# Outer norms of the mixing block and the memory attention computed by token halves, with GpSimd adding their residuals and squares

## The reference, cut to what matters

```python
x = x + rmsnorm(y @ w_out[l], g_mix_post[l])      # (1) mix_post
h = rmsnorm(x, g_mem_pre[l])                      # (1) mem_pre
y = memory_cross_attention(h, mem_n, w_mq[l], w_mk[l], w_mv[l], w_mo[l])
x = x + rmsnorm(y, g_mem_post[l])                 # (2) mem_post
h = rmsnorm(x, g_ff_pre[l])                       # (2) ff_pre
y = jnp.square(jax.nn.relu(h @ w_ff1[l])) @ w_ff2[l]
x = x + rmsnorm(y, g_ff_post[l])
```

## Time and profile before

| | us |
|---|---|
| median of 3 runs (2120.17 to 2122.87) | 2120.91 |
| profiled execution: time | 2122.2 |
| profiled execution: span of the core | 2120.4 |
| seam 1, last two blocks of w_out to the closing of mem_pre | 309.67 to 353.66 |
| seam 2, last two blocks of w_mo to the closing of ff_pre | 440.78 to 484.77 |

### The profile page before, as it was taken

How to read it: one execution, slowest core, us unless ns; L and a number is a source line. 1 busy time by engine, 2 the same in 40 slices (tenths; PEclk the granted TensorE clock), 3 DMA queues, 4 the chain that set the end, 5 groups by cost and what they waited for, 6 DMA issues and landing times.

```text
span 2120.4 us, 27323 instructions
## 1 busy us (share of the span) xinstructions
PE 2074.9 (98%) x11100; PEld 1665.4 (79%) x11100; DVE 1243.8 (59%) x1943; ACT 836.3 (39%) x1362; POOL 210.8 (10%) x182
## 2 busy tenths in 40 slices
PE   8999999999999999999999999999999999999998
PEld 7787977678878886666988888887777779888887
DVE  5566746446677777986644344475675756443443
ACT  5345544445323233225523223354464455232232
POOL 1321011011000004552000000100000010000002
PEclk9999999999999999999999999999999999999999
DMA  6313422016677762763232333121121232323331
GB/s 203 116 53 100 150 93 86 20 60 217 219 278 255 260 232 90 181 166 93 97 104 96 100 100 100 54 70 51 60 70 51 70 106 94 104 96 100 100 100 40
DMA packets 219710, 245.56 MB, mean 116 GB/s; under 512 B 9272, under 2 KB 205368, under 8 KB 213440
## 3 DMA queue, kind: packets, MB, share of 16 engines
q1 hardware_dynamic: 209360, 231.20, 33.3%
q10 hardware_dynamic: 10224, 12.61, 2.3%
HBM read 237.75 MB, written 3.78 MB: 114 GB/s over the span
## 4 chain that ended last, share of the span: by engine, by line
PE 88%; DVE 5%; ACT 3%; DMA 2%; issue 1%; ACTq 0%; POOL 0%; DVEq 0%; SPq 0%
PE bank L1420 24%; PE bank L1424 24%; PE bank L1428 24%; PE bank L1446 2%; PE bank L1454 2%; PE bank L1450 2%; PE bank L1556 1%; PE bank L1630 1%; DVE wL L2039 1%; PE bank L1607 1%; PE bank L1514 1%; PE bank L1491 1%; PE bank L1499 1%; ACT wH L1666 1%; PE bank L1620 1%
## 5 line engine op out<-in xcount | busy, mean ns | idle before, releaser
L1420 PE MATMUL bank<-hH,wH 128*128 128x512 f32 (+1 forms) x1768 | 643.7, 385 | 15.8 <-ACT wH L1671 7.9
L1428 PE MATMUL bank<-hL,wH 128*128 128x512 f32 (+1 forms) x1768 | 627.0, 375 | 0.0
L1424 PE MATMUL bank<-hH,wL 128*128 128x512 f32 (+1 forms) x1768 | 626.5, 375 | 0.0
L1666 ACT ACTIVATE wH<-raw 128x1024 fp32r<-128x1024 f32 (+1 forms) x376 | 333.8, 937 | 365.3 <-PE bank L1428 293.1
L2039 DVE TENSOR_TENSOR wL<-raw,wH 128x1024 fp32r<-128x1024 f32 (+1 forms) x340 | 378.8, 1151 | 136.3 <-ACT wH L1666 136.2
L1420 PEld LDWEIGHTS bank<-hH,wH 128*128 128x128 f32 x1768 | 326.6, 189 | 101.7 <-issue 28.0
L1428 PEld LDWEIGHTS bank<-hL,wH 128*128 128x128 f32 x1768 | 327.1, 189 | 60.7
L1424 PEld LDWEIGHTS bank<-hH,wL 128*128 128x128 f32 x1768 | 326.9, 189 | 60.0 <-issue 3.1
L1420 PE MATMUL bank<-hidH,wH 128*128 128x512 f32 (+1 forms) x800 | 305.1, 381 | 1.9 <-ACT hidH L1830 1.9
L1428 PE MATMUL bank<-hidL,wH 128*128 128x512 f32 (+1 forms) x800 | 304.6, 381 | 0.0
L1424 PE MATMUL bank<-hidH,wL 128*128 128x512 f32 (+1 forms) x800 | 304.4, 381 | 0.0
(11 more groups left out here) (220 smaller groups left out, 2037.1 us busy)
## 6 DMA issues: line engine op xcount, KB each, us to landing
raw<-in_mlp SPq DMA_DIRECT2D x64, 1024.0 KB, 5.3
araw<-in_ada_w SPq DMA_DIRECT2D x48, 1024.0 KB, 5.1
raw<-in_w_ff SPq DMA_DIRECT2D x32, 1024.0 KB, 7.3
raw<-in_hgrn_in SPq DMA_DIRECT2D x32, 512.0 KB, 3.7
raw<-in_w_in SPq DMA_DIRECT2D x11, 1024.0 KB, 5.2
raw<-in_conv_in SPq DMA_DIRECT2D x16, 512.0 KB, 3.9
u<-conv_u ACTq DMA_DIRECT2D x24, 270.0 KB, 5.1
raw<-in_w_mv SPq DMA_DIRECT2D x4, 1024.0 KB, 5.0
```

What stands on the lines that cost most here:

```text
L1420: mm(out, wH[:, s, m:m + 128], xh[:, k, c], start=k == 0, stop=False)
L1424: mm(out, wL[:, s, m:m + 128], xh[:, k, c], start=False, stop=False)
L1428: i = mm(out, wH[:, s, m:m + 128], xl[:, k, c], start=False, stop=k == KB - 1)
L1666: do(wH[:, s, c], raw[:, r, c], ACT.Copy).then_inc(*s_whi.up(n, x))
```

## The change

Both seams get the halved form; `post_norm` replaces the second branch of `post_pre`. All eight `post_x` of both halves go to POOL. All eight squares of the next norm are put off until the second half has been scaled, and all seven additions go to POOL. The three useless matmuls go from these two closings. `beside` is called after `between` and the next weight's high part. Half keys are renamed from 0 to "a", which changes no instruction. Left out below are the same half slices in `ev_block`, `pre_hi`, `pre_lo` and `post`.

```diff
@@ linear @@
-            if self.beside is not None:
-                self.beside()
-                self.beside = None
...
                     if k == 1:
                         between()
                         self.highs(ns[0] + NSPLIT)
+                        if self.beside is not None:
+                            self.beside()
+                            self.beside = None
@@ post_pre, post_norm @@
-            self.close(tag, 1024, busy=BUSY)
-            add = {}
-            for j in range(KB):
-                self.do("post", tag=tag, src=src, j=j, rb=None, z=None)
-                if j:
-                    self.do("pre_lo", tag=tag, nxt=nxt, j=j - 1)
-                self.do("post_x", tag=tag, src=src, j=j, pool=False, z=None)
-                self.do("pre_hi", tag=tag, nxt=nxt, j=j)
-                if j < 4:
-                    self.to_add = None
-                    self.square(nxt, j, ("xT", j), (self.x_event(tag, j),), by="dve")
-                    add[j + 2], self.to_add = self.to_add, None
-                if add.get(j) is not None:
-                    self.do("add_square", **add[j])
-            self.do("pre_lo", tag=tag, nxt=nxt, j=KB - 1)
-
-            def rest():
-                for j in range(4, KB):
-                    self.square(nxt, j, ("xT", j), (self.x_event(tag, j),))
-            self.beside = rest
+    def post_norm(self, tag, nxt):
+
+        def scale(half):
+            for j in range(KB):
+                self.do("post", tag=tag, src="ymix", j=j, rb=None, z=None, half=half)
+                if j:
+                    self.do("pre_lo", tag=tag, nxt=nxt, j=j - 1, half=half)
+                self.do("post_x", tag=tag, src="ymix", j=j, pool=True, z=None, half=half)
+                self.do("pre_hi", tag=tag, nxt=nxt, j=j, half=half)
+                yield
+            self.do("pre_lo", tag=tag, nxt=nxt, j=KB - 1, half=half)
+
+        def squares():
+            for j in range(KB):
+                self.square(nxt, j, ("xT", j), (self.x_event(tag, j),))
+
+        def second():
+            self.close_half(tag, 1024, 1)
+            run(scale(1))
+            self.rstd_free = (("dve", "post", tag, KB - 1),)
+            self.beside = squares
+
+        return dict(close=lambda half: self.close_half(tag, 1024, half), scale=scale, second=second)
@@ build @@
-        run(self.linear("w_out", "w_out", 0, 0, 1024, ("h", "y"), to_block("mix_post"), fresh=2))
-        self.post_pre("mix_post", "mem_pre", "ymix")
+        mem_pre, ff_pre = self.post_norm("mix_post", "mem_pre"), self.post_norm("mem_post", "ff_pre")
+        run(self.linear("w_out", "w_out", 0, 0, 768, ("h", "y"), to_block("mix_post"), fresh=2))
+        run(self.seam("w_out", "w_out", 0, 0, ("h", "y"), to_block("mix_post"), mem_pre))
...
         run(self.linear("mq", "w_mq", 0, 0, 1024, ("h", "mem_pre"), to_mq,
-                        before=lambda: self.close("mem_pre", 1024), fresh=4, hold=5))
+                        before=lambda: self.close("mem_pre", 1024), fresh=4, hold=5, between=mem_pre["second"]))
...
-        run(self.linear("w_mo", "w_mo", 0, 0, 1024, ("h", "mo"), to_block("mem_post"), fresh=2))
-        self.post_pre("mem_post", "ff_pre", "ymix")
+        run(self.linear("w_mo", "w_mo", 0, 0, 768, ("h", "mo"), to_block("mem_post"), fresh=2))
+        run(self.seam("w_mo", "w_mo", 0, 0, ("h", "mo"), to_block("mem_post"), ff_pre))
...
-        run(weave(self.ffn("ff_pre", "w_ff1", 0, "w_ff2", 0, ("h", "ff_pre"), True, to_y), ada(), RM, start=-12.0))
-        self.post_pre("ff_post", None, "yff")
+        run(weave(self.ffn("ff_pre", "w_ff1", 0, "w_ff2", 0, ("h", "ff_pre"), True, to_y, between=ff_pre["second"]), ada(), RM,
+                  start=-12.0))
+        self.post_pre("ff_post", "yff")
@@ pool_program, post_x @@
-                    e.tensor_tensor(xT[:, j, :], xT[:, j, :], y, ADD).then_inc(*s_pool.up("x", tag, j))
+                    e.tensor_tensor(xT[:, j, c], xT[:, j, c], block(it["src"], j)[:, c], ADD).then_inc(
+                        *s_pool.up("x", tag, j, *end))
```

More of the change, by code:

```diff
@@ L176, in cols @@
         return slice(0, T), ()
-    return (slice(0, T // 2), (0,)) if half == 0 else (slice(T // 2, T), ())
+    return (slice(0, T // 2), ("a",)) if half == 0 else (slice(T // 2, T), ())
 class Schedule:
@@ L401, in close_half @@
                 rstd_free=() if half else self.rstd_free, out=out, half=half)
[L402 removed]
+        self.lin.put(b, ("act", "ln", tag, *cols(half)[1]))
         if half:
@@ new lines, in second, with post_pre @@
+        def second():
[4 more added lines that the diff above has]
+        return dict(close=lambda half: self.close_half(tag, 1024, half), scale=scale, second=second)
+    def post_pre(self, tag, src):
+        rb, free = self.lin.get()
+        self.close(tag, 1024, busy=BUSY, out=(rb, free))
+        for j in range(KB):
+            pool = j in BY_POOL
+            z, free = (None, ()) if pool else self.lin.get()
+            self.do("post", tag=tag, src=src, j=j, rb=rb, z=z, after=free, half=None)
+            self.do("post_x", tag=tag, src=src, j=j, pool=pool, z=z, half=None)
+            if not pool:
+                self.lin.put(z, ("dve", "x", tag, j))
+        for j in range(KB):
+            self.square_mm(tag, j)
+        self.lin.put(rb, ("dve", "post", tag, KB - 1))
@@ L562, in scale @@
     def scale(self, tag, before, half):
-        end = (0,) if half == 0 else ()
+        end = cols(half)[1]
         held = None
@@ L1435, in tensor_program @@
                     wl = wL[:, n % NSPLIT, :].rearrange("p (b n) -> p b n", b=KB)
-                    ready = (0,) if it.get("half") == 0 else ()
+                    ready = cols(it.get("half"))[1]
                     for k in it["ks"]:
@@ L2163, in vector_program @@
                     tag, j = it["tag"], it["j"]
[L2164 to L2166 removed]
+                    c, end = cols(it["half"])
+                    y = block(it["src"], j)[:, c]
+                    dve.wait_ge(*s_act.at("rstd", tag, *end))
+                    dve.wait_ge(*(s_dve.at("y", 3, j) if tag == "ff_post" else s_act.at("y", tag, j, *(end if j >= KB - 2 else ()))))
                     for ev in it.get("after", ()):
                         dve.wait_ge(*event(ev))
[L2169 to L2171 removed]
+                    e.scalar_tensor_tensor(out=y if it["z"] is None else banks[it["z"]][:, c], in0=y, scalar=vc(GAIN[tag], j),
+                                           in1=rstd[:, c] if it["rb"] is None else banks[it["rb"]][:, c], op0=MUL,
+                                           op1=MUL).then_inc(*s_dve.up("post", tag, j, *end))
                 elif kind == "post_x" and not it["pool"]:
@@ L2174, in vector_program @@
                     dve.wait_ge(*s_dve.at("post", tag, j))
[L2175 to L2178, removed]
+                    dve.wait_ge(*event(plan.x_event("mem_post", j)))
                     z = block(it["src"], j) if it["z"] is None else banks[it["z"]][:]
                     e.tensor_tensor(xT[:, j, :], xT[:, j, :], z, ADD).then_inc(*s_dve.up("x", tag, j))
[L2181 to L2185, removed]
                 elif kind == "pre_lo":
                     j = it["j"]
[L2188 to L2191, removed]
+                    c, end = cols(it["half"])
+                    dve.wait_ge(*s_hi.at(it["nxt"], j, *end))
+                    dve.wait_ge(*event((*plan.x_event(it["tag"], j), *end)))
+                    e.scalar_tensor_tensor(out=hL[:, j, c], in0=xT[:, j, c], scalar=vc(GAIN[it["nxt"]], j),
+                                           in1=hH[:, j, c].bitcast(F), op0=MUL, op1=SUB).then_inc(
+                        *s_lo.up(it["nxt"], j, *end))
                 elif kind == "ev_mq":
@@ L2480, in pool_program @@
                     tag, j = it["tag"], it["j"]
-                    y = block(it["src"], j)
-                    pool.wait_ge(*s_dve.at("post", tag, j))
+                    c, end = cols(it["half"])
+                    pool.wait_ge(*s_dve.at("post", tag, j, *end))
                     if tag == "mix_post":
```

38 lines of the change are left out of this document (13 added, 25 removed).

## The result

The changed kernel takes 2136.93 us (median of 5 runs, 2134.21 to 2137.81), the kernel before 2120.91 us (median of 5, 2120.17 to 2122.87). The ratio is 1.0068, with a 95% interval of 1.0057 to 1.0079: the change makes the kernel slower by 12 to 17 us. The prediction said 2133.5 us in a range of 2121.5 to 2138, with 80% for slower. The profiled execution has a span of 2132.3 us.

A forecast was written before the change was run, and what follows sets the result against it. PE, busy 98% of the span, was taken as the bound. Per seam +5.7 us (late closing) and +0.6 (clock) gave +6.3, for both +12.6 on the median 2120.91: 2133.5 us, range 2121.5 to 2138.

The forecast's parts named there:

- What bounds: At two seams: PE is busy 98% of the span, so its idle time and number of matmuls decide the change's worth.
- PE alone: Per seam, without waits: mem_pre's closing sum at t = 41.4 from block 5's end instead of 43.99, a gain of 2.6 us.
- The first half's chain: In each seam: DVE, POOL and ACT need 1.42 us a block against PE's 1.44; PE waits 0.8 us at second closing.
- The start of the additions: Late in each seam, after the squares begin: POOL starts the first of seven additions at t = 37.2; last ends at 49.6.
- The closing: Next norm's closing sum: PE, there at t = 42.2, waits for POOL until 49.7, 5.7 us later than 43.99.
- The clock: After PE's wait at each seam's closing: a fall of the granted clock costs 0.6 us, bounds 0 and 1.4.
- The sum: Both seams: +5.7 and +0.6 make +6.3 us a seam, +12.6 in all, giving 2133.5 us.
- PE alone decides: Rival, 7%: POOL is ready for both closings and PE runs through; -2.6 us a seam, 2115.8 us.
- The turns at the end: From the fourth addition, POOL additions and DVE low parts alternate, 2.25 us a pair; rival lacking turns or hold-up: 12%, 2127.2.
- the hold-up within the chains: In halved chains, a DVE operation behind a POOL one loses 0.5 us; rival lacking this or the turns: 12%, 2127.2.

The follow-up runs named there:

- the repeat: The changed kernel measured once more, unaltered, beside the kernel before: 2138.51 us against 2123.77, ratio 1.0069.
- the filled one: The changed kernel plus seven useless matmuls ahead of the closing sums of mem_pre and ff_pre, in PE's wait: 2135.22 us, ratio 1.0055; again 2134.01, ratio 1.0052.

## Why the prediction was right

- **What bounds**: right. PE's idle time at two places decided it; with the additions off GpSimd the rest of the change gains, and with the additions alone the kernel loses.
- **PE alone**: predicted t = 41.4 for a closing without waits, measured 41.96. The narrow matmuls cost what the earlier trace rows gave (7.20 us to the first sum, to the digit). Of the 0.56 us missing, 0.2 lie in the second halved sum, 0.90 us instead of 0.68, and the rest in small steps before and behind it.
- **The first half's chain**: of the 0.8 us of wait at the second closing only those 0.2 came. The square of block 7 started at 323.79, t = 15.4, where I had 15.9: the first `post` started at t = 9.2 instead of 9.4, and ACT, POOL and DVE each handed on a little sooner than I had written out. The block's distance was 1.42 us in the sum and 1.39 in the trace. The hold-up of DVE came out at 0.47 to 0.48 us, as in the earlier trace rows (`post` of 0.95 and 0.96 us beside an addition), and not at POOL's whole 0.73. The Trainium skill says that the two engines exclude each other, and for the whole instruction (SBUF — State Buffer, "Who interferes with whom"), and the trace agrees: each `post` that is held up ends 0.28 to 0.29 us behind POOL's addition, as here at 325.37 and 325.08. What DVE loses is what is left of the addition when DVE gets to its own instruction. The prediction had read the rule as a loss of the whole 0.73 us, 1.53 a block; that doesn't follow from it.

```profile
324.18 0.90 POOL L2488 TENSOR_TENSOR xT<-xT,vt 128x256 f32<-128x256 f32 x1 [0.84 <-DVE vt L2176]
324.42 0.95 DVE L2176 SCALAR_TENSOR_TENSOR vt<-vt,vec,rstd 128x256 f32<-128x256 f32 x1
```

- **The start of the additions**: t = 37.2 predicted, 36.1 measured (344.46), the same small steps added up (Ln of the second half at t = 21.0 instead of 21.6, its first `post` at 21.9 instead of 22.7). Their length: 12.4 us predicted, 12.50 measured, with the turns. The last one ended 1.0 us sooner than I had it, and that is the error of this term.
- **The closing**: +5.7 us a seam predicted, +4.7 measured.
- **The clock**: the term that was mis-sized. I put 0.6 us a seam, between bounds of 0 and 1.4 from the earlier trace rows. It cost 3.8 and 2.4 us in one execution, 2.4 twice in the other. I had reasoned that part of a short low phase would lie within the wait. But the phases were 13.7 and 10.2 us long, where the one of the earlier trace rows lasts 3.4, and 9 and 6 us of them lay behind the wait:

```profile
352.53:366.19 13.66, 8.25 (x17) 5.37 (x18) 8.59 (x8) 1.32 (x2) 4.14 (x3) 0.50 0.46 154
492.48:502.70 10.22, 5.04 (x9) 2.91 (x10) 6.77 (x6) 2.80 (x5) 4.06 (x2) 0.50 0.62 205
```

- **The sum**: 12.6 us predicted. The seams lost 15.8 and, in the repeat, 14.3 us (7.16 + 7.13); the medians moved by 16.0 and 14.7. Two errors of opposite sign, -1.0 a seam for the start of the additions and +1.8 to +3.2 for the clock, left 2 to 3 us. That the time lies this near to the forecast is in part luck.
- **The rivals**: the runs without additions on GpSimd show the case "PE alone decides" as it would have been, at t = 41.96 and a gain of 3.9 us; I had put 5.1. With the additions on DVE it was 3.6 and 4.7 us, and 5.5 with the residual additions there too. The turns at the end did come, and the hold-up within the chains as well.

## What to carry to other kernels

When a step is moved off a busy engine, ask for whom it is the last input, and add up the queue that it joins up to that moment: seven additions of 1.3 us, the last three made in turns with another engine's work and the first started 36 us into a stretch of 42, can't be done in time, however idle GpSimd is on average. A new wait of PE of some us should be priced with the low clock behind it, and that from a row with a wait of the same length. A halved norm saves its wait only if the next norm's sum is ready when PE, now sooner there, asks for it.

## What the runs showed of the hardware that I had not expected

The low clock lasts longer than the gap in which it begins: with gaps of 6.6 us it lasted 13.7 us once and 10.2 us five times (six seams of three traces), with the gaps of 3.1 us 6.8 us both times. PE had been running at 1.2 GHz for up to 9 us by the time it rose.

And falls occur where nothing was changed. Leaving out the low clock at the very end, which every trace has, the kernel before has two, at 825.5 and 972.3; the changed kernel has one behind seam 2, at 840.6; the filled one three in its first trace and two in its second. The three:

```profile
608.70:612.10 3.40, 3.40 (x9) 2.62 (x9) 3.40 (x4) 0.81 (x1) 0.00 (x0) 0.51 1.12 388
837.40:840.80 3.40, 3.39 (x4) 1.49 (x5) 3.33 (x6) 1.66 (x4) 2.63 (x3) 0.51 0.00 0
984.20:987.60 3.40, 3.40 (x10) 2.62 (x9) 3.40 (x7) 2.12 (x5) 0.00 (x0) 0.52 0.00 0
```

The rest behind seam 2 (from the first matmul of the second feed-forward product to the end) follows their number in all eleven traces of this study: 1614.4 to 1615.7 us with one fall, 1616.6 to 1617.6 with two, 1619.9 with three. Each of these falls stands at one of three idle stretches of PE, of 1.87, 3.27 and 2.37 us, which are in all eleven traces and bring a fall in 6, 8 and 6 of them. Two more such places lie ahead: one of 1.07 us near 203 us, with a fall in 4 traces, and one of 1.65 us between the seams, with a fall in 3 of the four traces whose clock fell in seam 1, and in no other (70.55 us between the seams instead of 68.84). So the length of a gap alone doesn't tell whether the clock falls, two executions of one kernel can differ by such a fall, and a single profile can't tell a gain of 0.1% from it. What decides whether one of these falls occurs wasn't tried, nor whether the edit has a part in it.
